# An attention and expert-mixing block on one core: latent weights asked for later, the first query's scores in two banks, the second tile's latent transposes moved

## The reference

```
xn = rms_norm(x, norm1_g);  parts = xn @ w_in           # queries, keys, values, gates, latents
o_nsa = nsa_attention(...)                               # compressed + selected + windowed keys
o_mla = mla_attention(c_q, c_kv, k_rope, ...)            # latent attention, 8 heads
merged = sigmoid(gate_nsa) * (o_nsa @ w_branch_nsa) + sigmoid(gate_mla) * (o_mla @ w_branch_mla)
h = x + merged @ w_out
q = rms_norm(h, norm2_g) @ w_query                       # 8 heads, two halves of 128 each
s1, s2 = q[..., 0, :] @ sub_keys_1.T, q[..., 1, :] @ sub_keys_2.T
v1, i1 = top_k(s1, 16);  v2, i2 = top_k(s2, 16)          # 128 keys each
top_s, pos = top_k(v1[:, None] + v2[None, :], 16)        # 16 of the 256 sums
e = i1 * 128 + i2 at pos;  g = softmax(top_s)
y = sum over heads and picks of g * gelu(expert_down[e] . xn2) * expert_up[e]
out = rms_norm(h + y, norm_f_g)
```

## Time and profile before

| what | us |
|---|---|
| median of 3 runs | 969.05 |
| lowest, highest | 964.12, 970.46 |
| the profiled execution | 965.61 |
| its span, first to last instruction | 963.8 |
| TensorE busy | 781.4 (81%) |
| VectorE busy | 554.7 (58%) |
| ScalarE busy | 173.9 (18%) |
| GpSimd busy | 587.7 (61%) |
| mean DMA rate over the span | 321 GB/s |

### The profile page before, as it was taken

One profiled execution on the slowest core, in us unless ns is written; L12 is line 12 of the kernel. 1 busy time (PEld: TensorE's weight loads), 2 busy tenths in 40 slices (PEclk: granted clock), 3 DMA queues, 4 the chain that ended last, 5 costly groups with the idle time before them and its releaser, 6 DMA issues.

```text
span 963.8 us, 8830 instructions
## 1 busy us (share of the span) xinstructions
PE 781.4 (81%) x2504; PEld 420.9 (44%) x2504; DVE 554.7 (58%) x1457; ACT 173.9 (18%) x536; POOL 587.7 (61%) x721
## 2 busy tenths in 40 slices
PE   8999999999798497778958576978784988677685
PEld 5988778565453243334423233333332443222231
DVE  2455565258897565655565565665655665654434
ACT  2232433100311102030202020202020211101001
POOL 7875341036676666666666666666666767667673
PEclk9999999999999799989899988989898999999999
DMA  9945431749999999999999989999999999999995
GB/s 269 227 155 207 153 157 45 291 170 371 373 364 355 346 378 359 393 342 364 354 373 337 411 305 375 361 368 365 363 351 385 337 387 373 343 386 364 349 407 212
DMA packets 103735, 308.98 MB, mean 321 GB/s; under 512 B 22672, under 2 KB 27536, under 8 KB 103696
## 3 DMA queue, kind: packets, MB, share of 16 engines
q0 software_dynamic: 73792, 268.48, 73.8%
q1 hardware_dynamic: 24768, 39.91, 12.1%
q10 hardware_dynamic: 5136, 0.15, 0.4%
HBM read 306.93 MB, written 1.05 MB: 320 GB/s over the span
## 4 chain that ended last, share of the span: by engine, by line
PE 44%; another core or an unknown queue 18%; POOL 14%; issue 9%; DVE 6%; DMA 5%; ACT 1%; ACTq 1%; POOLq 0%; SPq 0%; DVEq 0%
PE bank L1455 39%; POOL region_w L618 10%; DMA region_w<-in_expert_up,chosen 4%; PE xn_ps L1455 3%; PE bank L1458 2%; POOL gates L618 2%; DVE region_w L1350 1%; ACTq L705 1%; POOL pool_bd L618 1%; DVE gates L1350 1%; DMA region_w<-in_expert_down,chosen 1%; POOL dn_spare L618 1%; DMA x_sb<-in_x 0%; ACT pool_bd L867 0%
## 5 line engine op out<-in xcount | busy, mean ns | idle before, releaser
L1455 PE MATMUL bank<-region_w,pool_bd 128*128 128x512 f32 (+2 forms) x1004 | 482.5, 623 | 80.0 <-DMA region_w<-in_expert_up,chosen 56.9
L1455 PEld LDWEIGHTS bank<-region_w,pool_bd 128*128 128x128 f32 x1004 | 191.0, 201 | 343.1 <-issue 305.4
L618 POOL DMA_INDIRECT region_w<-in_expert_up,chosen x250 | 238.5, 954 | 162.4 <-issue 62.1
L1350 DVE CUSTOM_DVE_ANT_0 region_w<-xn_ps,region_w 128x1024 f32<-128x1024 f32 x128 | 156.4, 1223 | 139.9 <-DMA region_w<-in_expert_down,chosen 130.0
L618 POOL DMA_INDIRECT region_w<-in_expert_down,chosen x128 | 121.4, 948 | 40.1 <-issue 35.7
L867 ACT ACTIVATE pool_bd<-ident,pool_bd 128x128 f32<-128x128 f32 x250 | 82.6, 392 | 206.4 <-PE bank L1455 122.2
L1350 DVE CUSTOM_DVE_ANT_0 gates<-xn_ps,gates 128x1024 f32<-128x1024 f32 x64 | 78.0, 1221 | 47.1 <-DMA gates<-in_expert_down,chosen 41.2
L687 ACT ACTIVATE pool_bd<-bank 128x256 f32<-128x256 f32 (+3 forms) x49 | 19.0, 389 | 341.5 <-remote 236.5
L618 POOL DMA_INDIRECT gates<-in_expert_down,chosen x64 | 63.7, 995 | 23.5 <-issue 17.7
L1458 PE MATMUL bank<-ident,pool_bd 128*128 128x128 f32 x30 | 8.9, 394 | 80.8 <-ACT pool_bd L687 43.3
L1455 PE MATMUL bank<-region_q,oT 128*128 (+1 forms) x240 | 54.6, 379 | 1.9 <-issue 1.7
(11 more groups left out here) (275 smaller groups left out, 832.4 us busy)
## 6 DMA issues: line engine op xcount, KB each, us to landing
region_q<-in_w_in SPq DMA_DIRECT2D x4, 2048.0 KB, 8.3
region_q<-in_w_query SPq DMA_DIRECT2D x1, 6144.0 KB, 22.5
region_w<-in_expert_up,chosen POOLq DMA_INDIRECT x250
region_w<-in_w_out SPq DMA_DIRECT2D x1, 3072.0 KB, 20.8
x_sb<-in_x SPq DMA_DIRECT2D x4, 512.0 KB, 4.2
region_q<-in_w_in SPq DMA_DIRECT2D x2, 1024.0 KB, 10.8
region_q<-in_w_in SPq DMA_DIRECT2D x16, 128.0 KB, 3.0
region_w<-in_wb_nsa SPq DMA_DIRECT2D x1, 2048.0 KB, 14.1
```

Of the source, the lines that this page charges most:

```text
L618: pool.indirect_dma_start(out=row, out_offset=None, in_=table, in_offset=bass.IndirectOffsetOnAxis(ap=chosen[s % PICKS][:, k:k + 1], axis= ...
L1350: dve.tensor_tensor_reduce(out=row, in0=xn_ps[:, :], in1=row, scale=1.0, scalar=0.0, op0=ALU.mult, op1=ALU.add, accum_out=hdn[s % 2][:, k: ...
L1455: return pe.matmul(out_, lhsT, rhs, start=start, stop=stop)
```

## The change

There are three edits.

One: SyncE asks for the latent weights when the first half of block 1 has landed (`win1_in[0]`), instead of the last load of block 0; and for `w_query` when three `outputT` copies and all attention value products (`pv_mm`) are done, instead of four copies.

Two: the first query's scores are formed half by half. `first_keys(0)` writes to bank 6 and counts in the new semaphore `first_key`, `first_keys(1)` writes to bank 7 and counts in `key_mm`. VectorE searches each half on its own wait. As bank 6 holds scores until VectorE has read them, the second query product waits for `keys_read` 1 instead of `qt_cp` 1.

Three: `outputT(3)` goes from behind `branch(0, 0)` to behind `back(0, xn_in)`, with a wait for `h_ready` 2, as bank 3 has been used by `w_out_part` in between; its copy on ScalarE goes behind the copy of the query's first half. The wait for `o_done` 6 that came with it is now ahead of the fourth branch product.

```diff
-            sp.wait_ge(win0_in[KC - 1], 16)
+            sp.wait_ge(win1_in[0], 16)
             sp.dma_start(w_uq, a["w_uq"].rearrange("(k p) n -> p k n", p=P)).then_inc(mla_w_in, 16)
...
-            sp.wait_ge(ot_cp, 4)
+            sp.wait_ge(ot_cp, 3)
+            sp.wait_ge(pv_mm, len(UNITS))
             query_columns = a["w_query"].rearrange("(k p) n -> p k n", p=P)
...
-            for b in range(4):
+            def outputT_copy(b):
                 act.wait_ge(ot_mm, b + 1)
...
+            for b in range(3):
+                outputT_copy(b)
...
             first_query_copy()
+            outputT_copy(3)
             softmax_exp(0)
...
+        first_scores = [banks[6][:, 256:256 + P], banks[7][:, P:2 * P]]
...
-                keys = [banks[7][:, half * NK:(half + 1) * NK] for half in range(2)]
+                keys = first_scores if p == 0 else [banks[7][:, half * NK:(half + 1) * NK] for half in range(2)]
...
-                dve.wait_ge(key_mm, p + 1)
-                for half in range(2):
-                    own.mark(dve.max(top_v[:, half, best], keys[half]))
+                if p == 0:
+                    dve.wait_ge(first_key, 1)
+                    own.mark(dve.max(top_v[:, 0, best], keys[0]))
+                    dve.wait_ge(key_mm, 1)
+                    own.mark(dve.max(top_v[:, 1, best], keys[1]))
+                else:
+                    dve.wait_ge(key_mm, p + 1)
+                    for half in range(2):
+                        own.mark(dve.max(top_v[:, half, best], keys[half]))
...
                 pe.wait_ge(o_done, b + 3)
+                if b == 3:
+                    pe.wait_ge(h_ready, 2)
...
                 if p == 1:
-                    pe.wait_ge(qt_cp, 1)
+                    pe.wait_ge(keys_read, 1)
...
+            def first_keys(half):
+
+                if half == 0:
+                    pe.wait_ge(qt_cp, 1)
+                mm(first_scores[half], q_T[:, half * P:(half + 1) * P], skT[:, half * P:(half + 1) * P]).then_inc((first_key, key_mm)[half], 1)
...
             branch(0, 0)
-            pe.wait_ge(pt_cp, N)
-            outputT(3)
             branch(0, 1)
             branch(0, 2)
             pe.wait_ge(ot_cp, 3)
+            pe.wait_ge(o_done, 6)
...
             first_query(1, 1)
+            first_keys(0)
             pe.wait_ge(qd_cp, 1)
-            key_scores(0)
+            first_keys(1)
             back(0, xn_in)
+            outputT(3)
             branch(1, 0)
```

More of the change, by code:

```diff
@@ L305, in block_program @@
         q_mm, q_cp, qt_mm, qt_cp, key_mm = (sem(n) for n in ("q_mm", "q_cp", "qt_mm", "qt_cp", "key_mm"))
-        qd_cp = sem("qd_cp")
+        qd_cp, first_key = sem("qd_cp"), sem("first_key")
         keys_read, top_ready, exp_ready, soft_ready = (sem(n) for n in ("keys_read", "top_ready", "exp_ready", "soft_ready"))
```

## The result

The changed kernel takes 975.63 us (median of 20 runs), the kernel before 967.29 (20 runs): ratio 1.008, 95% interval 1.0056 to 1.0105. It is some 8 us slower, where 968.8 was forecast with a range to 971.8. That is under the 1% that the forecast called measurable, but a ratio of 1 lies outside the interval, and no step of the sum stands behind the loss. One of the 20 runs took 1550.74 us, which nothing here explains; it doesn't move the median. The profiled execution took 978.14 us, 2.5 over the median; its span is 976.3, against 963.8 before, so these two traces lie 12.5 us apart where the medians lie 8.3.

What follows compares the result with a forecast made beforehand. Taken as bound by DMA in the expert-row gathers, whose start hangs on TensorE. Four gathers come 0.91 us sooner, the rest 0.22; only -0.22 us reaches the end: 968.8 us against the median 969.05, range 964.5 to 971.8.

Steps and rivals of the forecast that it cites:

- the transposes come back: Second tile's four latent transposes, moved behind the search, cost the same 0.44 us ahead of y_mm 6 and y_mm 8.
- key product: First half's key product runs in TensorE's idle 0.38 us before the search, so TensorE gets through 0.22 us sooner.
- a late signal that grows instead of vanishing: Rival: the delay of y_mm 8's signal at the fourteenth gather lengthens; no size; 0.08 shared with the slower new-wait case.
- an assumed hold of 5 us: In the slower rival, VectorE's search held 5 us by an unseen cause: y_mm 8 2.95 us later less 0.22, 971.8 us.
- the new wait: TensorE's second query product waits for keys_read: cover 2.05 us, cost 0; as slower rival, 0.08 including a longer delay.
- a late signal goes away: Rival: y_mm 8's delay at the fourteenth gather vanishes, later gathers come up to 2.2 us earlier, 967.6 us; chance 0.07.
- transfers at the chip's pace: Stream of expert-row gathers: about 730 of the 963.8 us, whose number and size the change doesn't touch.
- the delay stays: At the fourteenth gather: products may simply end later than drawn, so the 2.49 us idle would remain; left undecided.
- The front: Latent weights' later request, early blocks: taken as 0, kept between -0.3 and +1 us; 0.3 or more had chance 0.03.
- the query weights: Requested 3.9 us earlier, but already landing before their use, with no gather running yet: gain 0.
- the estimate of 1.1 us for the four: Four latent transposes at the skill's about 275 ns each, worth 1.1 us at the first gather instead of 0.44.
- The sum of -0.22 us: Shift of the kernel's end: the first four gathers' 0.91 us is not kept, only y_mm 8's 0.22 us remains.

Runs made afterwards that it cites:

- the stall at the merged products: Changed kernel with the products for the second tile's merged transposes, first half, made seven times instead of once (11.2 us more of TensorE): ratio 1.0197 to before.
- the stall in before: Kernel before with the products for the second tile's merged transposes, first half, made seven times instead of once (11.2 us more of TensorE): ratio 1.0234.

## Why the prediction was wrong

**The failing step** is "the transposes come back ... There they cost the same 0.44 us", with the sum "-0.44 (transposes gone) - 0.22 (key product) + 0.44 (transposes back)". It took each row's duration as a property of the instruction that stays when its neighbours move. Where TensorE runs at its pace this is right: the fortieth gather shifts by 0.4 us. Where it has slow stretches the move measured +8.3 us at the fortieth gather, counted from the first, instead of 0.44 (65.3 us against 57.0), and 12 us in time (2 to 22), with the transposes moved alone. That the moved work sets off a longer slow stretch is shown by the traces; by which property of it (0.44 us more work there, the copy, an unbroken queue) stays open.

**The rival that came true** stood in one sentence: "a late signal that grows instead of vanishing, which can't be told beforehand". It had no price of its own; the upper end of the range, 971.8, came from an assumed hold of 5 us, and 0.08 stood for it and the new wait together. A single copy of the second tile came 10.7 us later behind the first gather (30.4 us against 19.7). Its sibling, "a late signal goes away", came true as well and at the same time: y_mm 8 was on time, but the delay had moved to the next products and grown. I weighed them as alternatives. The 2.49 us at the fourteenth gather was the edge of one slow stretch, and the two copies behind it, with 6.80 and 4.56 us put down to remote, stood in the same trace; I priced only the first, since it alone held a gather. A single wait of 35.3 us put down to remote on ScalarE was there to be read as well. TensorE's rows in that trace have 16 gaps of over 2.5 us, 94.6 us in all, where before on chip 0 has none, and the two spans are 75 us apart. The statement that about 730 us are "transfers at the chip's pace" was wrong: by the pace that the same engines hold in their best stretches (409 GB/s) it would be 656.

The Trainium skill, Perfetto Trace Analysis, Summary: the profiler window per engine type, was cited for matmul ends being estimates and signal travel hidden. The traces agree (a copy at 237.20 behind matmuls drawn to 227.4), and the conclusion that I drew in the next sentence, "the delay stays", did not follow.

**The front** was forecast at 0, with at most 0.3 us to gain, and gave about 1.2 in the first pair of traces: ScalarE's queue ends at 19.27 instead of 21.65, and TensorE's second product starts at 21.18 instead of 22.35. "TensorE is then the later one" was right, but only the wait of 0.35 us was counted; the last part of the first product itself started 0.66 us earlier (12.80 against 13.46), perhaps because the blocks that feed it no longer shared the DMA engines with the latent weights. The pair overstates what can be known: the second product starts between 20.60 and 23.52 in the traces with the first edit, and between 21.54 and 23.09 in those without it. With the first edit alone the time falls by 0.09% (0 to 0.18%); between the changed kernel with and without it, in different sessions, by 0.2%.

**Right** were: the query weights (0), key products in TensorE's idle time, the fifth gather's idle time at 1.18 us (1.2 forecast), no wait at the second query product (212.66 follows at once), and the first gather 0.91 us sooner by the parts behind the front. This last one stands in every trace: from the second product's start to the first gather all traces with that part of before take 186.5 us, those with the halves alone 186.1, with the transposes alone 186.0 to 186.1, and those with both 185.6 to 185.7. The four transposes take 0.44 us in their new place too (205.36 to 205.80); one matmul row of theirs is drawn as 0.27 us long, but they start 0.11 us apart, so the estimate of 1.1 us for the four took a duration for a cost. The sum of -0.22 us for all but the front stands beside 0.9999 (0.9990 to 1.0008), on the kind of chip where it applies.

**The test lines** caught it: "the fourteenth gather off by over 1 us" and "the stretch from 250 us on longer ... by more than 2 us" were named as what no step gives, and both came.

## What to carry to other kernels

A wait that a trace puts down to something it doesn't know, behind an instruction drawn as done, is a result that came late. Look for such waits on all engines, and for gaps in TensorE's rows, before calling the kernel bound by DMA, and treat an edit that moves TensorE's work near them as open to some 8 us, where its own count says tenths. The sum of such waits is no measure of the loss: here 216.5 of 236.5 us would have been waited without them as well. An edit worth tenths of a microsecond should be timed on more than one chip, since here its sign changed between them. A profile of the kernel before on each tells which of the two cases is being tuned for.

## What the runs showed of the hardware

- The same program takes 890 us on chips 0, 1 and 9 and 970 on chips 14 and 15. Granted clock 0.999 against 0.943, DMA 409 against 366 GB/s in the stream; the first 208 us of before agree to 0.3 us between one trace of either kind, less than two executions on one kind can differ (208.9 and 209.6). What sets them apart, the chips or what runs beside them, was not found.
- On the second kind TensorE has slow stretches, up to some 15 us long if the longest gaps in its rows are such (14.5 us in before, 13.5 in the changed kernel, 14.9 in it with the stall at the merged products). No wait ahead of 205 us is put down to remote in any trace; all come behind the first gather, where the DMA engines are nearly full. TensorE slows by more than the clock: 0.58 us a pass, where 0.12 is usual. The granted clock comes after: with the stall in before it falls at 235.8, 3 us into the slow passes; in the changed kernel it falls to its lower level (1.2 GHz) at about 230 us, when no matmul is drawn behind 227.4, and is back at 2.4 GHz before 245.
- VectorE is late there too, more seldom: the changed kernel's first trace has 16 waits, 31.1 us in all, in which VectorE waits for a signal of its own that came up to 5.5 us after the drawn end; before has 5 (9.7 us), and the traces of both on chip 0 have none.
- Up to the first merged copy these stretches repeat across chips for the same order of instructions (19.7, 19.8 and 19.7 us behind the first gather; 30.4, 30.4, 30.6 and, once, 32.0), and they change when 0.44 us of transposes move.
